# Modulation chunks 4 to 11 on the vector engine, and gate products around the attention transposes, in a two-layer transformer kernel

## What is computed

```python
mod = silu(c) @ w_mod[l] + b_mod[l]              # (1, 6144)
sh_m, sc_m, g_m, sh_f, sc_f, g_f = split(mod, 6)
h = rms_norm(x) * (1 + sc_m) + sh_m
x = x + g_m * mixer(h, ...)                      # three branches, each gated, then w_out
h = rms_norm(x) * (1 + sc_f) + sh_f
x = x + g_f * moe_ffn(h, ...)                    # 64 experts, top 8, and a shared one
```

## Time and profile before

| | |
|---|---|
| median of 3 runs | 2196.98 us (2195.28 to 2197.26) |
| the profiled execution | 2196.92 us, of which its span is 2195.2 us |
| PE / PEld busy | 2087.9 us (95%) / 1253.4 us (57%) |
| DVE / ACT / POOL busy | 886.8 (40%) / 434.4 (20%) / 59.4 us (3%) |
| mean granted TensorE clock | 0.983 |

### The profile page before, as it was taken

One profiled execution on the slowest core, in us unless ns is written; L12 is line 12 of the kernel. 1 busy time (PEld: TensorE's weight loads), 2 busy tenths in 40 slices (PEclk: granted clock), 3 DMA queues, 4 the chain that ended last, 5 costly groups with the idle time before them and its releaser, 6 DMA issues. The chain is left out here.

```text
span 2195.2 us, 34081 instructions
## 1 busy us (share of the span) xinstructions
PE 2087.9 (95%) x13140; PEld 1253.4 (57%) x13140; DVE 886.8 (40%) x1930; ACT 434.4 (20%) x945; POOL 59.4 (3%) x143
## 2 busy tenths in 40 slices
PE   5999999899999999979999998999999998799998
PEld 3844444566666666666444445666666665366475
DVE  2674422533333333329643134333333332253253
ACT  2233112011111111113221011111111111113131
POOL 1000001100000000000000030000000000110000
PEclk9999999999999999999999989999999999899999
DMA  9652837599999999855536426999999998531721
GB/s 330 201 210 84 306 115 283 214 401 400 396 399 404 400 395 398 341 197 185 199 109 236 183 105 266 388 405 391 410 391 400 402 394 311 173 96 43 229 71 56
DMA packets 165286, 599.13 MB, mean 273 GB/s; under 512 B 13052, under 2 KB 17760, under 8 KB 130656
## 3 DMA queue, kind: packets, MB, share of 16 engines
q1 hardware_dynamic: 163808, 595.10, 71.1%
q0 software_dynamic: 1408, 3.10, 0.7%
HBM read 597.11 MB, written 1.05 MB: 272 GB/s over the span
## 5 line engine op out<-in xcount | busy, mean ns | idle before, releaser
L1199 PE MATMUL banks<-weight_ring,h_t 128*64 128x256 f32 x4224 | 481.8, 381 | 3.2 <-DVE h_t L1947 3.2
L1199 PEld LDWEIGHTS banks<-weight_ring,h_t 128*64 128x64 f32 x4224 | 298.3, 137 | 173.9 <-issue 38.2
L850 PE MATMUL banks<-weight_ring,h_t 128*128 128x512 f32 x768 | 337.5, 596 | 4.1 <-issue 1.8
L850 PEld LDWEIGHTS banks<-weight_ring,h_t 128*128 128x128 f32 x768 | 145.7, 191 | 188.8 <-issue 184.1
L1187 PEld LDWEIGHTS banks<-z,sp_ 128*128 128x128 bf16 x3168 | 178.8, 98 | 55.8 <-issue 49.2
L1187 PE MATMUL banks<-z,sp_ 128*128 128x128 bf16 x3168 | 201.1, 220 | 4.9 <-DVEq L1937 4.9
L1973 DVE SCALAR_TENSOR_TENSOR o_parts<-banks,slot_weight,o_parts 128x512 fp32r<-128x512 f32 x132 | 99.1, 751 | 246.3 <-ACT o_parts L1504 246.3
L1953 DVE TENSOR_TENSOR z<-banks,z 128x128 f32<-128x128 f32 x132 | 38.5, 292 | 318.9 <-ACT z L1489 318.9
L1504 ACT ACTIVATE o_parts<-banks,slot_weight 128x512 fp32r<-128x512 f32 x132 | 90.7, 687 | 295.4 <-PE banks L1226 295.4
L1239 PE MATMUL banks<-o_parts,slot_of 128*128 128x512 f32 x528 | 141.2, 410 | 6.9 <-issue 6.9
L2202 PE MATMUL banks<-weight_ring,h_t 128*128 128x512 f32 (+2 forms) x384 | 135.6, 513 | 2.9 <-ACTq L2378 2.9
(11 more groups left out here) (465 smaller groups left out, 1876.7 us busy)
## 6 DMA issues: line engine op xcount, KB each, us to landing
weight_ring<-in_w SPq DMA_DIRECT2D x264, 1024.0 KB, 10.7
weight_ring<-in_w_in SPq DMA_DIRECT2D x36, 2048.0 KB, 11.8
slots<-in_w SPq DMA_DIRECT2D x68, 1024.0 KB, 8.5
weight_ring<-in_w_mod SPq DMA_DIRECT2D x24, 2048.0 KB, 10.1
qk<-in_w SPq DMA_DIRECT2D x32, 1024.0 KB, 7.2
z<-in_w SPq DMA_DIRECT2D x32, 1024.0 KB, 12.1
weight_ring<-in_w_out SPq DMA_DIRECT2D x8, 2048.0 KB, 8.0
weight_ring<-in_w_in SPq DMA_DIRECT2D x10, 1024.0 KB, 7.8
```

Of the source, the lines that this page charges most:

```text
L850: mm = nc.tensor.matmul(bank[:, 0:cols], stationary[:, k, t * P:(t + 1) * P], w[:, k, 0:cols], start=(k == 0), stop=(k == KT - 1))
L1199: mm = nc.tensor.matmul(h_bank[g * SLOTS:(g + 1) * SLOTS, 0:FF], x_blk[:, j // 2, k, own], w13(j)[:, :, k, g * (FF // 2):(g + 1) * (FF // 2)],
```

## The change

TensorE no longer multiplies chunks 4 to 11. VectorE does: `mod_on_dve` waits for the chunk's load, multiplies the first 128 x 512 piece by its column of `c_act`, and adds the seven others with a fused multiply and add, each behind a drain. TensorE's sum is now a matmul with ones over that buffer. The reader that frees a chunk's slot is now this VectorE work, and SyncE waits for it. The ring's list is reordered, as are the places of the sums. Branch 0's first two gate products (column half 0) stand on TensorE around the attention output's transposes. The next layer's parts 12 to 15 each move one place later.

```diff
 MOD_STEPS = {
-    "z": [("part", 4)], "qa": [("part", 5)], "ka": [("part", 6)],
-    "aT": [("sum", 4), ("sum", 5), ("part", 7), ("sum", 6)],
-    "oa": [("part", 8), ("sum", 7), ("part", 9), ("sum", 8), ("part", 10)],
-    "oaT": [("sum", 9), ("part", 11), ("sum", 10), ("sum", 11)],
+    "ka": [("sum", 4), ("sum", 5)], "va": [("sum", 6)], "aT": [("sum", 7), ("sum", 8), ("sum", 9)],
+    "merged": [("sum", 10), ("sum", 11)],
 }
-MOD_NEXT = {"merged": [("part", 12)], "mT": [("part", 13)], "wo": [("sum", 12), ("part", 14)],
-            "turned": [("sum", 13), ("part", 15)], "rt": [("sum", 14), ("sum", 15)]}
+DVE_CHUNKS = range(4, 12)
+MOD_NEXT = {"mT": [("part", 12)], "wo": [("part", 13), ("sum", 12)], "turned": [("part", 14), ("sum", 13)],
+            "rt": [("part", 15), ("sum", 14), ("sum", 15)]}
...
-        mod_chunks(*range(MOD_FIRST if first else 0)) + [(n, (n, 1)) for n in ("ug", "ua", "qc", "kc")]
-        + mod_chunks(4) + [("qa", ("qa", 1))] + mod_chunks(5) + [("ka", ("ka", 1))] + mod_chunks(6)
-        + [(n, (n, 1)) for n in ("vc", "va")] + branch_chunks(2) + mod_chunks(*range(7, MOD_CHUNKS))
-        + branch_chunks(0) + branch_chunks(1) + mod_chunks(*((12, 13) if following else ()))
-        + [(("wo", h), ("wo", h, 1)) for h in range(2)] + mod_chunks(*((14, 15) if following else ())) + [("shared", None)]
+        mod_chunks(*range(MOD_FIRST if first else 0)) + plain("ug", "ua") + mod_chunks(4, 5) + plain("qc", "kc", "qa")
+        + mod_chunks(6) + plain("ka", "vc", "va") + mod_chunks(7) + b2[:1] + mod_chunks(8) + b2[1:] + mod_chunks(9, 10)
+        + b0 + b1 + mod_chunks(11) + later(12) + wo(0) + later(13) + wo(1) + later(14, 15) + [("shared", None)]
...
+                    elif before is not None and before[0] == "mod_dve":
+                        sp.wait_ge(dve_parts.sem, dve_parts.at(l, before[1] - DVE_CHUNKS[0] + 1))
...
+                        elif c in DVE_CHUNKS:
+                            pe.wait_ge(dve_parts.sem, dve_parts.at(l, c - DVE_CHUNKS[0] + 1))
+                            mm = nc.tensor.matmul(bank[:], K.ones[:], mod_part[c], start=True, stop=True)
...
-                mod("oa")
+                branch_gate(0, 0, 0)
                 pe.wait_ge(oa_ready.sem, oa_ready.at(l))
...
-                mod("oaT")
-                for t in range(T):
-                    branch(0, 0, t)
+                branch_gate(0, 0, 1)
+                for t in range(T):
+                    branch_y(0, 0, t)
...
+                def mod_on_dve(c):
+                    dve.wait_ge(C[l]["mod", c].filled, C[l]["mod", c].filled_at(l))
+                    w = C[l]["mod", c].tile
+                    v.tensor_scalar(mod_part[c], w[:, 0, :], K.c_act[:, 0:1], None, ALU.mult)
+                    for k in range(1, KT):
+                        dve.drain()
+                        v.scalar_tensor_tensor(mod_part[c], w[:, k, :], K.c_act[:, k:k + 1], mod_part[c], ALU.mult, ALU.add)
+                    dve.drain().then_inc(dve_parts.sem, 1)
```

More of the change, by code:

```diff
@@ L376, in _groups_1 @@
         + [("z0", par, i) for par in range(2) for i in range(2)] + [("z1", par) for par in range(2)]
-        + mod_groups("z", layer) + [("qa", t) for t in range(T)] + mod_groups("qa", layer)
-        + [("ka", t) for t in range(T)] + mod_groups("ka", layer)
+        + [("qa", t) for t in range(T)] + [("ka", t) for t in range(T)] + mod_groups("ka", layer)
         + [("suf", r, par) for r in range(3) for par in range(2)]
-        + [(n, t) for n in ("vc", "va") for t in range(T)]
+        + [(n, t) for n in ("vc", "va") for t in range(T)] + mod_groups("va", layer)
         + [("oc", i) for i in range(2)]
@@ L385, in _groups_1 @@
         + [("aT1", i) for i in range(2)] + ["aT0"] + mod_groups("aT", layer)
-        + [("oa", t) for t in range(T)] + mod_groups("oa", layer) + [("oaT", i) for i in range(2)]
-        + mod_groups("oaT", layer)
-        + [x for t in range(T) for x in branch_groups(0, 0, t)] + ["cmean"]
+        + [("oa", t) for t in range(T)] + [("gt", 0, 0, 0)] + [("oaT", i) for i in range(2)] + [("gt", 0, 0, 1)]
+        + [("y", 0, 0, t) for t in range(T)] + ["cmean"]
         + branch_groups(0, 1, 0) + ["cvar"] + branch_groups(0, 1, 1)
@@ L402, in mod_chunks, with plain, wo, later @@
 def mod_chunks(*chunks):
-    return [(("mod", c), ("mod_part", c)) for c in chunks]
+    return [(("mod", c), ("mod_dve" if c in DVE_CHUNKS else "mod_part", c)) for c in chunks]
 def chunks_1(layer):
     first, following = layer == 0, layer + 1 < DEPTH
-    return (
-        mod_chunks(*range(MOD_FIRST if first else 0)) + [(n, (n, 1)) for n in ("ug", "ua", "qc", "kc")]
-        + mod_chunks(4) + [("qa", ("qa", 1))] + mod_chunks(5) + [("ka", ("ka", 1))] + mod_chunks(6)
-        + [(n, (n, 1)) for n in ("vc", "va")] + branch_chunks(2) + mod_chunks(*range(7, MOD_CHUNKS))
-        + branch_chunks(0) + branch_chunks(1) + mod_chunks(*((12, 13) if following else ()))
-        + [(("wo", h), ("wo", h, 1)) for h in range(2)] + mod_chunks(*((14, 15) if following else ())) + [("shared", None)]
+    def plain(*names):
+        return [(n, (n, 1)) for n in names]
+    def wo(h):
+        return [(("wo", h), ("wo", h, 1))]
+    def later(*chunks):
+        return mod_chunks(*(chunks if following else ()))
+    b2, b0, b1 = (branch_chunks(i) for i in BRANCHES)
+    return (
+        mod_chunks(*range(MOD_FIRST if first else 0)) + plain("ug", "ua") + mod_chunks(4, 5) + plain("qc", "kc", "qa")
+        + mod_chunks(6) + plain("ka", "vc", "va") + mod_chunks(7) + b2[:1] + mod_chunks(8) + b2[1:] + mod_chunks(9, 10)
+        + b0 + b1 + mod_chunks(11) + later(12) + wo(0) + later(13) + wo(1) + later(14, 15) + [("shared", None)]
     )
@@ L582, in first_block @@
         gate_loaded = signal("gate_bias_loaded", 16 * len(MOD_ROW_PARTS))
+        dve_parts = signal("mod_dve_parts", len(DVE_CHUNKS))
         x_mid, x_out = signal("x_after_mixer", T), signal("x_after_layer", T, T)
@@ L764, in _ @@
                         sp.wait_ge(sh_h_done.sem, sh_h_done.at(l, T))
+                    elif before[0] == "mod_dve":
+                        sp.wait_ge(dve_parts.sem, dve_parts.at(l, before[1] - DVE_CHUNKS[0] + 1))
                     else:
@@ L894, in mod, with branch_gate, branch_y @@
                         mm.then_inc(B[l]["mod_" + what, c].full, 1)
-                def branch(i, h, t):
+                def branch_gate(i, h, t):
+                    rows(("gt", i, h, t), l, chunk(("gt", i, h), l), t, K.h_t)
+                def branch_y(i, h, t):
                     feat, ready = ((oa_t, oat_ready), (yb_t, ybt_ready), (yc_t, qkt_ready))[i]
-                    rows(("gt", i, h, t), l, chunk(("gt", i, h), l), t, K.h_t)
                     w = chunk(("p", i), l).rearrange("p k n -> p (k n)").rearrange("p (k n) -> p k n", n=D)
@@ L907, in branch @@
                     mm.then_inc(B[l]["y", i, h, t].full, 1)
+                def branch(i, h, t):
+                    branch_gate(i, h, t)
+                    branch_y(i, h, t)
                 def by_rows(name):
@@ L952, in _ @@
                     mm.then_inc(B[l]["z1", par].full, 1)
-                mod("z")
                 by_rows("qa")
-                mod("qa")
                 by_rows("ka")
@@ L968, in _ @@
                 by_rows("va")
+                mod("va")
                 pe.wait_ge(v_ready.sem, v_ready.at(l))
@@ L1375, in _ @@
                 nc.scalar.activation(sp_[:], sp_[:], ACT.Ln, bias=1.0).then_inc(log_ready.sem, 1)
-                copy_mod(4)
                 for w, name in enumerate(("qa", "ka")):
@@ L1380, in _ @@
                         copy_out((name, t), l, qk[:, t, w * 512:(w + 1) * 512], bank[:])
-                    copy_mod(5 + w)
                 act.drain().then_inc(qk_ready.sem, 1)
@@ L1422, in _ @@
                 act.drain().then_inc(at_ready.sem, 1)
-                for c in (7, 8):
-                    copy_mod(c)
                 act.wait_ge(oa_sq_ready.sem, oa_sq_ready.at(l))
@@ L1427, in _ @@
                     .then_inc(oa_std_ready.sem, 1)
-                copy_mod(9)
+                gate_sig(0, 0, 0)
                 for i in range(2):
@@ L1432, in _ @@
                 act.drain().then_inc(oat_ready.sem, 1)
-                for c in (10, 11):
-                    copy_mod(c)
-                for h, t in ((0, 0), (0, 1), (1, 0)):
+                for h, t in ((0, 1), (1, 0)):
                     gate_sig(0, h, t)
@@ L1448, in _ @@
                 following = l + 1 < DEPTH
-                if following:
-                    copy_mod(12)
                 for g in range(4):
@@ L1455, in _ @@
                 if following:
-                    copy_mod(13)
+                    copy_mod(12)
                 row_norm(1, l)
                 if following:
-                    copy_mod(14)
+                    copy_mod(13)
                 modulate(1, l)
                 if following:
-                    copy_mod(15)
+                    copy_mod(14)
```

(29 more changed lines are left out.)

## The result

| | before | changed |
|---|---|---|
| median of 4 runs each | 2196.95 us | 2163.92 us (2162.91 to 2165.74) |
| ratio | | 0.9853, 95% interval 0.984 to 0.9865 |
| span of the profiled execution | 2195.2 us | 2162.2 us |
| PE / DVE / ACT busy | 2087.9 / 886.8 / 434.4 us | 2057.2 / 978.2 / 424.8 us |
| mean granted TensorE clock | 0.983 | 0.982 |

The kernel is 33.0 us faster; 35.3 us were forecast. DVE's busy time rose by 91.4 us, PE's fell by 30.7.

A forecast was written before the change was run, and what follows sets the result against it. PE was taken to bound the mixer. Layer 0's -20.0 and +7.3 and layer 1's -19.6 and -3.0 sum to -35.3 us, from 2196.9 to 2161.6 us, range 2157 to 2166.

The forecast's parts named there:

- The parts: TensorE's chunk multiplications in the mixer: removing eight a layer at 1.85 us each takes away 14.8 us.
- sums 4 and 5: TensorE sums of chunks 4 and 5, moved before the suffix sums at the same price: 1.9 us.
- The gate chunk of branch 2: Branch 2's second gate chunk, loaded into chunk 7's slot, lands late for PE: 0.2 us per layer, bounds 0 and 1.5.
- A DVE chunk: One chunk's multiply and seven multiply-adds on DVE with drains: 6.4 us, bounds 5.8 and 6.8; 102 us in all.
- rival 1: DVE chunks take about 9 us; PE stops 2.7 us longer at branch 2's second gate chunk: 2167 us, chance 0.12.
- From attention transposes to `cmean`: Mixer stretch through attention output and branch 0's gate products: saves 16.7 us in layer 0, 16.4 in layer 1.
- rival 3: Stop before branch 0's first gate product is longer or lowers the clock: 2.5 us more a layer, 2166.6; chance 0.15.
- Rival 5: Mixer: loads, not PE, bound it, so the change doesn't do what it says; about 2193 us, chance 0.03.
- The tail of layer 0: `wo` waits 4.0 us for its second half, 2.5 for the clock, 0.8 for a later part: +7.3 us.
- Part 15: Layer 0, between router product and shared expert: 1.85 us on PE, partly hidden; cost 0.8, bounds -1.3 and 1.9.
- The tail of layer 1: Two sums fill 1.9 us before the `merged` transposes and the clock stays up: -3.0 us, bounds 0 and -3.0.
- Rival 4: Mixer: DVE's chain sets PE; x us/chunk stops it x-6.1 (gate chunk) plus 3(x-9) (chunk 9's sum); 2203 at x=14; chance 0.03.

The follow-up runs named there:

- gates_not_moved: Changed kernel with branch 0's two gate products put back behind the output's transposes, chunks still on DVE: 2173.09 us, ratio 0.9888.
- wo_halves_together: Changed kernel with both halves of `wo` loaded one behind the other in layer 0, chunk 13 behind them: 2154.58 us, ratio 0.9798.
- changed_again: The changed kernel itself, unedited, measured again beside its variants on one chip: 2160.48 us, ratio 0.9828.
- gate_chunk_earlier: Changed kernel with branch 0's first gate chunk loaded ahead of chunk 10: 2151.57 us, ratio 0.9781.
- the last experiment: Kernel with both load orders, layer 1's sum 11 moved from before the `merged` transposes to behind `wo`: 2150.85 us, ratio 0.9782.
- both orders: Changed kernel with both `wo` halves ahead of chunk 13 and branch 0's first gate chunk ahead of chunk 10: 2150.42 us, ratio 0.978.
- doubled chunks: Changed kernel with each DVE chunk computed twice, the result the same: 2187.58 us, ratio 0.9961.
- gates_moved_alone: Kernel before the change with only branch 0's two gate products moved, parts and load order kept: 2214.74 us, ratio 1.0078.

## Why the prediction was right, point by point

- **The parts.** A part was put at 1.85 us. The stage to the suffix sums lost 4.13 us for three parts less and two sums more; with sums at 0.86 (133.05 to 133.91) a part is (4.13 + 1.72) / 3 = 1.95. The forecast for this and the next stage was -3.45 + 0.2 = -3.25, measured were -4.2. That is 0.9 us a layer too little, 0.3 from the parts, 0.2 from sums 4 and 5 (put at 1.9, measured 1.72), 0.4 from sum 6 and the gate chunk.
- **The gate chunk of branch 2.** Put at 0.2 us, measured none: issued at 191.50, wanted at 200.19, and landed after 8.2 us. Sum 6 cost nothing either.
- **A DVE chunk.** 6.4 us forecast, 6.46 measured, so rival 1 (9 us) falls. The Trainium skill, "VectorE: DVE Perf Modes", section "The DRAIN you can't avoid", would have made a step 1.23 us. The seven dependent multiply-adds of chunk 7 with their drains took 5.71 us, a step of (5.71 - 0.75) / 6 = 0.83 for an instruction of 0.75: no run here shows the flush of that rule. DVE's 91.4 us more of busy time are what the instructions show without drains; with them the forecast's 102 us stands.
- **From attention transposes to `cmean`.** -16.7 and -16.4 us forecast, -16.2 and -16.5 measured. The stop was put at 1.6 us and was 2.23 in layer 0 and 1.68 in layer 1; the bound was 1.9. The chunk landed 8.7 us after its issue (220.99 to 229.7), not 8.1 to 8.6, and PE was there after 6.7, not 6.9. The clock stayed up (7.13 us for the product), so rival 3 had only the 0.6 us in layer 0. Rival 5 (the loads bound the mixer) falls with it: what PE lost came off. `gates_not_moved` shows the cover to be real: 6.61 us of wait.
- **The tail of layer 0.** +7.3 forecast. The stop of 4.0 us was 3.71, and the clock's loss of 2.5 was 23.61 - 20.8 = 2.8: 6.5 of 6.5. The mechanism is settled by `wo_halves_together`; that the clock's part came so near is luck, as `changed_again` lost 1.4 us there and `gate_chunk_earlier` nothing. Part 15, put at 0.8 us, added 1.9 to the stage before the shared expert and the stage behind it was 2.2 shorter: its price is inside what the clock does there, and isn't known.
- **The tail of layer 1.** -3.0 forecast, -2.8 measured: -1.1 ahead of `wo` and -1.7 in it, as the clock stayed up.
- **Rival 4.** Its place was right (gate chunk of branch 2), but its second term can't be added to the first, as PE comes later by the first, and it lacked the bank of sum 4. At 12.8 us a chunk the kernel is still 0.4% below the time of before, as "slower only from about 13" had it.
- **The sum.** -20.0 + 7.3 = -12.7 in layer 0 became -14.0, -22.6 in layer 1 became -23.1. What the sum didn't hold are +4.1 us in stages that the change doesn't touch. In `changed_again`'s trace, with the same instructions, the start of layer 0 is 1.8 us earlier, layer 1's first products 1.7 and the end 2.8 us shorter: they vary from execution to execution, and the 2.3 us between forecast and median are less than that. So the mechanism and its places are borne out stage by stage; that the total came within 2.3 us is in part luck, 1.8 us more gain in the mixers against 4.1 us lost elsewhere.

## What to carry to other kernels

Work moved off the bound engine takes its cover along: look what its instructions hid (here 6.6 us of normalization in each layer), and put other ready work in the same place in the same change. A list of loads is part of the schedule: a use moved forward wants its load moved forward too, and a chunk that nobody needs yet must not stand between two halves that are used together. The ring's slots and the banks whose reader is on the newly loaded engine are where it became late first here, with that engine busy 49% of the time.

## What the runs showed of the hardware that I had not expected

- The clock after a stop isn't fixed by the stop. Behind the same stop of 3.7 us the 48 instructions of `wo` took 23.61, 22.28 and 20.87 us (granted clock 0.88, 0.94, 1.00). Stops of 2.23 and 1.68 us before a gate product cost nothing more. The 16 instructions of the norm's transposes in layer 1 took 1.16 + 1.16 us behind a stop of 2.75 us in `wo_halves_together`, 3.46 us behind one of 2.76 in `gate_chunk_earlier`, and 3.53 us behind one of 1.90 in the last experiment.
- The runs of one kernel spread by very different amounts: 2154 to 2165 us for the changed kernel (2163 to 2166 in the first measurement), 2147 to 2153 us with both orders, 2181 to 2195 us with doubled chunks. Long stops alone don't make this: `gates_not_moved`, with 6.61 us of stop in each layer, and `gates_moved_alone`, with 8.9, lie within 2.6 us in four runs each. What does is open.
- A drain between dependent fp32 multiply-adds of 128x512 on DVE costs 0.08 us in the chain of seven; in the pair before the change it was 0.09.
